# A last product in two column halves: its second pass split into two runs by token halves, and the final scaling of the output spread over GpSimd and ScalarE

## The chip, the cores and the metric

The kernel runs on one core of a Trainium2 chip. The metric is the device time of one execution in microseconds, smaller is better, given as the median of the runs. The change is judged against the kernel before.

## What is computed

One layer of a hybrid encoder for 512 tokens of width 2048: an RMS norm, one wide input projection, a sparse attention branch and a state-space branch, both gated and merged, then the output projection with the residual, and a final RMS norm. The change touches only the last two lines:

```python
def rms_norm(x, g):
    xf = x.astype(jnp.float32)
    y = xf * lax.rsqrt(jnp.mean(xf * xf, axis=-1, keepdims=True) + EPS)
    return (y * g.astype(jnp.float32)).astype(x.dtype)
...
    mixed = gates[:, :, 0] * y_a + gates[:, :, 1] * y_b
    return x + mixed @ w_out        # (512, 2048) @ (2048, 2048)
...
    return rms_norm(x, g_final)
```

## The kernel before, in words

Everything up to `mixed` streams weights through three slots and is the same in both kernels. "The last product" is `mixed @ w_out`. It is computed for one half of the output columns (1024) after the other. In each half the tokens, the inner dimension and the columns are each cut in two, and the 2x2 block product is made with seven block products instead of eight (Winograd's form): sums of blocks of `mixed` (`sums_of`) and sums of blocks of `w_out` (`w_sums` in HBM, made earlier by GpSimd's transfers) are multiplied, and the seven results are combined. A float32 operand is split in a high part (ScalarE copies it, `high_of_quarters`, L1058) and a low part (VectorE subtracts, `low_of_quarters`, L1570), and every block product of 128 rows by 512 columns is three matmuls (`block_product`, L752 to L754).

A block product has eight steps k over the inner dimension. Four pairs of PSUM banks hold the running results, one bank of a pair for each token tile `tb` (0, 1) of a token half: `a_banks` (shown as banks0), `b_banks` (banks2), `c_banks` (banks4), `d_banks` (banks6). Weights come in quarters of 128x512; a ring holds twelve. SyncE issues the load of a quarter when TensorE is done with the one twelve quarters back (`free_at`), ScalarE and VectorE split it, TensorE uses it. SyncE, ScalarE, VectorE and TensorE each run through the steps n in order, and extra work is hung on certain steps of their queues.

Per column half there is a **first pass**, 8 steps with 3 quarters and 18 matmuls each (into a, b, c), and a **second pass**, 8 steps with 4 quarters and 24 matmuls each (d, a, b, c). At the end of the first pass a is saved (`kept1`) and combined with b and c on VectorE (`mix`: u2, u4). The products a, b and c of the second pass wait for these. `add_shared` adds kept1, u2 and u4 to `res`, which holds x (`load_res`, one of eight loads a step from n = 10 on); it is eight additions on VectorE and stands at step 15 and at step 27. After column half 0 `take_first_half` adds the banks to `res` with ten additions at step 17 (L1596); the first matmul into each bank of column half 1 waits for `bank_taken`.

At the end, tiles of 128 tokens are finished in the order `LAST_TOKENS` = 2, 3, 0, 1. Columns 0 to 1023 of each tile are complete long before; they have been squared and multiplied by g_final. The last two steps run in the order b, d, then a, c, so tiles 2 and 3 are complete 24 matmuls before the end and tiles 0 and 1 at the end. For each tile ScalarE makes sum of squares and square root, VectorE the reciprocal (L1666) and the scaled second column half (`finish`, L1668), GpSimd scales the first column half (L497), and SyncE stores the two halves (L447, L449).

## Time and profile before

| what | value |
|---|---|
| median of 3 runs | 1167.07 us (1166.68 to 1168.58) |
| profiled execution, its own time | 1165.59 us |
| its span, first to last instruction | 1163.7 us |
| TensorE matmuls busy | 1129.8 us, 97% of the span |
| VectorE, ScalarE, GpSimd busy | 728.6, 427.9, 47.1 us |
| chain that ended last | TensorE 83%, VectorE 12%, ScalarE 2% |

An engine's share of busy time is an average. Where TensorE is full, other engines' work costs nothing, and only its gaps and the stretch after its last matmul can be shortened. The last product begins at 995.0 us of the span. Times of rows count from the start of the span.

### The profile page before, as it was taken

The page shows a single profiled execution, that of the slowest core. Times are in us where ns is not written, and L with a number is a line of the kernel's source. Part 1 is how long each engine was busy: PE and PEld are TensorE (multiplying, and loading weights), DVE is VectorE, ACT ScalarE, POOL GpSimd, SP SyncE. Part 2 cuts the span into 40 slices and gives each one's busy share as a digit, 9 for nine tenths or more (in the row PEclk, how much of TensorE's full clock was granted, in tenths as well). Part 3 has the DMA queues.
Part 4 walks back from the last instruction along what each step waited for, and adds up shares of the span by engine and source line. Part 5 has one row for each costly group of instructions (what it writes and reads, how often), then busy time and mean ns, then how long its engine had stood idle before and what let it go on. Part 6 is the DMA issues. An engine that isn't in the chain of part 4 may idle for free.

```text
span 1163.7 us, 13431 instructions
## 1 busy us (share of the span) xinstructions
PE 1129.8 (97%) x5381; PEld 934.4 (80%) x5381; DVE 728.6 (63%) x1227; ACT 427.9 (37%) x563; POOL 47.1 (4%) x48
## 2 busy tenths in 40 slices
PE   5999999999999999999999999999999999999995
PEld 4999888888787788888777777888888888787884
DVE  5887558999646556528768886343234344866576
ACT  7423334332255452223222323333412222744363
POOL 4000000000000000000000000000000000000002
PEclk9999999999999999999999999999999999999998
DMA  7344443556633127565445656354576333578654
GB/s 252 102 116 109 142 148 109 138 116 140 150 109 97 50 76 171 143 134 154 130 122 160 144 127 149 115 179 145 113 165 156 78 103 90 182 241 288 216 187 170
DMA packets 188631, 166.35 MB, mean 143 GB/s; under 512 B 12868, under 2 KB 162712, under 8 KB 187928
## 3 DMA queue, kind: packets, MB, share of 16 engines
q1 hardware_dynamic: 167584, 129.97, 38.3%
q0 software_dynamic: 12800, 33.56, 12.7%
q10 hardware_dynamic: 8184, 1.95, 0.8%
q8 instruction: 43, 0.70, 0.2%
q14 instruction: 20, 0.16, 0.0%
HBM read 159.17 MB, written 37.75 MB: 169 GB/s over the span
## 4 chain that ended last, share of the span: by engine, by line
PE 83%; DVE 12%; ACT 2%; issue 1%; DMA 0%; ACTq 0%; POOL 0%; POOLq 0%; DVEq 0%
PE banks L507 21%; PE banks L508 21%; PE banks L509 21%; PE banks L752 4%; PE banks L753 4%; PE banks L754 4%; DVE w_lo L1154 2%; DVE score L1260 2%; DVE small L1259 2%; PE banks L659 2%; PE banks L640 1%; DVE score L1248 1%; DVE res L1596 1%; PE banks L709 1%; PE banks L649 1%
## 5 line engine op out<-in xcount | busy, mean ns | idle before, releaser
L507 PE MATMUL banks<-act_hi,w_hi 128*128 128x512 f32 (+1 forms) x1088 | 421.6, 388 | 2.7 <-DVE w_lo L1154 2.7
L509 PE MATMUL banks<-act_hi,w_lo 128*128 128x512 f32 (+1 forms) x1088 | 416.8, 383 | 0.0
L508 PE MATMUL banks<-act_lo,w_hi 128*128 128x512 f32 (+1 forms) x1088 | 416.7, 383 | 0.0
L1154 DVE TENSOR_TENSOR w_lo<-w_raw,w_hi 128x2048 fp32r<-128x2048 f32 x80 | 183.1, 2289 | 96.0 <-ACT w_hi L818 95.0
L507 PEld LDWEIGHTS banks<-act_hi,w_hi 128*128 128x128 f32 x1088 | 204.4, 188 | 42.9 <-DVE w_lo L1154 4.3
L509 PEld LDWEIGHTS banks<-act_hi,w_lo 128*128 128x128 f32 x1088 | 204.2, 188 | 38.5
L508 PEld LDWEIGHTS banks<-act_lo,w_hi 128*128 128x128 f32 x1088 | 204.5, 188 | 34.4
L818 ACT ACTIVATE w_hi<-w_raw 128x2048 fp32r<-128x2048 f32 (+1 forms) x81 | 154.2, 1903 | 101.5 <-DMA w_raw<-in_w_in 101.2
L1570 DVE TENSOR_TENSOR w_lo<-w_raw,w_hi 128x512 fp32r<-128x512 f32 (+1 forms) x64 | 68.2, 1088 | 43.6 <-ACT w_hi L1058 43.2
L1058 ACT ACTIVATE w_hi<-w_raw 128x512 fp32r<-128x512 f32 (+1 forms) x64 | 60.0, 951 | 72.6 <-DMA w_raw<-w_sums 48.7
L1583 DVE TENSOR_TENSOR gate<-gate,yb 128x512 f32<-128x512 f32 x16 | 11.1, 692 | 83.0 <-ACT gate L824 83.0
L824 ACT ACTIVATE gate<-banks,g_cols 128x512 f32<-128x512 f32 x16 | 11.0, 688 | 127.8 <-PE banks L509 127.8
L890 ACT ACTIVATE relu<-banks 128x256 f32<-128x256 f32 (+2 forms) x48 | 23.6, 492 | 90.8 <-PE banks L608 84.6
L507 PE MATMUL banks<-a_hi,w_hi 128*128 128x512 f32 x128 | 50.1, 391 | 0.0
L509 PE MATMUL banks<-a_hi,w_lo 128*128 128x512 f32 x128 | 49.8, 389 | 0.0
L508 PE MATMUL banks<-a_lo,w_hi 128*128 128x512 f32 x128 | 49.8, 389 | 0.0
L1248 DVE SCALAR_TENSOR_TENSOR score<-relu,w_idx,score 128x256 f32<-128x256 f32 (+2 forms) x45 | 27.8, 618 | 28.9 <-ACT relu L890 27.6
L754 PE MATMUL banks<-w_hi,ya_r 128*128 128x512 f32 x96 | 37.4, 389 | 0.0
L752 PE MATMUL banks<-w_hi,act_hi 128*128 128x512 f32 x96 | 37.3, 389 | 0.0
L753 PE MATMUL banks<-w_lo,act_hi 128*128 128x512 f32 x96 | 37.3, 389 | 0.0
L909 ACT ACTIVATE probs<-probs,small 128x128 f32<-128x128 f32 (+3 forms) x32 | 18.0, 563 | 42.7 <-DVE small L1352 42.7
L824 ACT ACTIVATE ya<-banks 128x512 f32<-128x512 f32 x16 | 9.6, 597 | 62.2 <-PE banks L509 53.3
(290 smaller groups left out, 1438.4 us busy)
## 6 DMA issues: line engine op xcount, KB each, us to landing
w_raw<-in_w_in SPq DMA_DIRECT2D x68, 1024.0 KB, 5.9
w_sums<-in_w_out POOLq DMA_DIRECT2D x24, 1024.0 KB, 8.4
w_raw<-w_sums SPq DMA_DIRECT2D x32, 512.0 KB, 4.2
w_sums<-w_sums POOLq DMA_DIRECT2D x8, 1024.0 KB, 11.2
w_raw<-in_w_att_out SPq DMA_DIRECT2D x8, 1024.0 KB, 5.5
w_raw<-in_w_out SPq DMA_DIRECT2D x16, 512.0 KB, 4.3
xt<-in_x SPq DMA_DIRECT2D x4, 1024.0 KB, 8.2
w_raw<-in_w_ssm_out SPq DMA_DIRECT2D x4, 1024.0 KB, 5.2
```

The lines of the kernel that those rows point to most:

```text
L507: nc.tensor.matmul(out_ap, wh, x_hi[k], start=(j == 0), stop=False)
L508: nc.tensor.matmul(out_ap, wh, x_lo[k], start=False, stop=False)
L509: last = nc.tensor.matmul(out_ap, wl, x_hi[k], start=False, stop=(j == n - 1))
L752: nc.tensor.matmul(bank[:, :], m_hi, hi_ring[:, w], start=(k == 0), stop=False)
L753: nc.tensor.matmul(bank[:, :], m_hi, lo_ring[:, w], start=False, stop=False)
L754: return nc.tensor.matmul(bank[:, :], m_lo, hi_ring[:, w], start=False, stop=(k == HALF_K - 1))
L818: nc.scalar.activation(w_hi[:, u % SLOTS, 0:n_el], w_raw[:, u % SLOTS, 0:n_el], ACT.Copy).then_inc(high_done, 1)
L890: nc.scalar.activation(relu[:, n % 2, 0:(b + 1) * P], pair_bank[n % 2][:, 0:(b + 1) * P], ACT.Relu, scale=IDX_DIM ** -0.5).then_inc(relu_d ...
L1058: nc.scalar.activation(hi_ring[:, part], raw_ring[:, part], ACT.Copy).then_inc(q_high, 1)
L1154: v.tensor_tensor(w_lo[:, u % SLOTS, :], w_raw[:, u % SLOTS, :], w_hi[:, u % SLOTS, :].bitcast(F32), ALU.subtract).then_inc(split_done, 1)
L1248: ins = v.scalar_tensor_tensor(scores[b], r, w, scores[b], ALU.mult, ALU.add)
L1570: v.tensor_tensor(lo_ring[:, part], raw_ring[:, part], hi_ring[:, part].bitcast(F32), ALU.subtract).then_inc(q_split, 1)
```

## The change

Steps are renumbered: each column half now has three **runs** of eight steps, named (half, run, k) here. Run 0 is the first pass as before. Run 1 has 2 quarters a step and makes the products of d and b, which belong to tiles 2 and 3; its steps go in pairs, d of both, then b of both. Run 2 has 2 quarters a step and makes a and c, which belong to tiles 0 and 1; in its last two steps all products of tile 0 come first and then all of tile 1. What hung on steps is hung on new ones: `load_res` on (0,1,4) to (0,2,3), `add_shared` on (0,2,1) and (1,1,3), the additions of d and b (`take_late_tokens`, six) on (half,2,4), those of a and c of column half 0 (`take_early_tokens`, four) on (1,0,1), ScalarE's means and square root table on (1,1,6), the finishing of tiles 2 and 3 on (1,2,5) and (1,2,6). The first step of column half 1 starts with b instead of a. The first column half of the last tile (tile 1) is scaled by ScalarE (`scale_half`), the other three by GpSimd as before. The number of matmuls, of bytes loaded and of bytes stored stays the same.

```diff
+def step_at(n):
+
+    half, run, k = n // (3 * HALF_K), n // HALF_K % 3, n % HALF_K
+    return half, run, k
...
-    return half * 7 * HALF_K + (3 * HALF_K + 4 * k if second else 3 * k)
+    half, run, k = step_at(n)
+    return half * 7 * HALF_K + (3 * k, 3 * HALF_K + 2 * k, 5 * HALF_K + 2 * k)[run]
...
-    return ((0, 2), (2, 4)) if block_at(n)[1] else ((0, 1), (1, 3))
+    return ((0, 2),) if step_at(n)[1] else ((0, 1), (1, 3))
...
+        def first_order(half, k):
+
+            return (1, 0, 2) if (half, k) == (1, 0) else (0, 1, 2)
...
-                if which == 1 - second:
-                    source = w_sums[half, k, :, 2 * second:2 * second + 2, :].rearrange("p i n -> p (i n)")
+                if which or run == 1:
+                    source = w_sums[half, k, :, 2 * run:2 * run + 2, :].rearrange("p i n -> p (i n)")
...
-                if 10 <= n < 18:
-                    if n == 10:
+                if 12 <= n < 20:
+                    if n == 12:
                         sp.wait_ge(m_low, 2 * HALF_K)
-                    load_res((n - 10) // TOK, (n - 10) % TOK)
-                if n == 3 * HALF_K:
-                    sp.wait_ge(q_done, done_at(2 * HALF_K + QUADS - 1, 2, 1))
+                    load_res((n - 12) // TOK, (n - 12) % TOK)
+                if n == 4 * HALF_K:
+                    sp.wait_ge(q_done, done_at(3 * HALF_K + QUADS - 1, 2, 1))
...
-            for i, t in enumerate(LAST_TOKENS):
+            for i, t in enumerate(LAST_TOKENS[:-1]):
                 pool.wait_ge(scale_ready, i + 1)
```
```diff
+            pe.wait_ge(tile_free, TILE0["out"])
+            for half in range(2):
+                n0 = half * 3 * HALF_K
+                for k in range(HALF_K):
+                    if half == 0:
+                        pe.wait_ge(m_low, SPLIT_ORDER.index((0, k)) + 1)
+                    for part in first_order(half, k):
+                        wait_quarter(n0 + k, part)
                         for tb in range(2):
-                            second_pass(n, i, tb).then_inc(q_done, 1)
+                            first_run(n0 + k, part, tb)
+                n0 += HALF_K
+                for k0 in range(0, HALF_K, 2):
+                    for part in range(2):
+                        for k in (k0, k0 + 1):
+                            if half == 0:
+                                pe.wait_ge(m_low, SPLIT_ORDER.index((1, k)) + 1)
+                            wait_quarter(n0 + k, part)
+                            for tb in range(2):
+                                second_run(n0 + k, part, tb)
+                n0 += HALF_K
+                for k in range(HALF_K - 2):
+                    wait_quarter(n0 + k, 0)
+                    for part in range(2):
+                        for tb in range(2):
+                            third_run(n0 + k, part, tb)
+                for tb in range(2):
+                    for k in (HALF_K - 2, HALF_K - 1):
+                        wait_quarter(n0 + k, 0)
+                        for part in range(2):
+                            third_run(n0 + k, part, tb)
```
```diff
             high_of_first(4)
 
+            def scale_half(i):
+                t = LAST_TOKENS[i]
+                act.wait_ge(scale_ready, i + 1)
+                act.wait_ge(first_scaled, 2 * TOK)
+                act.wait_ge(final_done, i)
+                nc.scalar.activation(res[:, t, 0:HALF], res[:, t, 0:HALF], ACT.Copy, scale=small[:, 188 + t:189 + t]
+                                     ).then_inc(final_done, 1)
...
+            def root_of(i):
+                t = LAST_TOKENS[i]
+                act.wait_ge(part_ready, i + 1)
+                link(nc.scalar.activation(square_out[:, 0:2, :].rearrange("p a n -> p (a n)"), res[:, t, HALF:D], ACT.Square,
+                                          accum_out=small[:, 176 + t:177 + t]))
+                nc.scalar.activation(small[:, 184 + t:185 + t], small[:, 176 + t:177 + t], ACT.Sqrt, bias=small[:, 180 + t:181 + t],
+                                     scale=1.0 / D).then_inc(squares_done, 1)
...
+                if half and run == 1 and k == 6:
+                    act.wait_ge(first_squared, 2 * TOK)
+                    for t in range(TOK):
+                        link(mean_of(t))
+                    link(nc.scalar.activation(small[:, 176:177], small[:, 163:164], ACT.Sqrt))
+                if half and run == 2 and k in (5, 6):
+                    root_of(k - 5)
+            for i in (2, 3):
+                root_of(i)
+            scale_half(3)
```
```diff
-            def take_first_half():
-
-                n = 2 * HALF_K - 1
-                dve.wait_ge(shared_added, 8)
+            def finished(half, run, part, tb):
+
+                dve.wait_ge(q_done, done_at(3 * HALF_K * half + HALF_K * run + HALF_K - 1, part, tb))
+
+            def take_late_tokens(half):
+
+                dve.wait_ge(shared_added, 8 * half + 8)
+                col = half * HALF
                 for tb in range(2):
-                    dve.wait_ge(q_done, done_at(n, 1, tb))
-                    add_part(tb, 0, a_banks[tb]).then_inc(bank_taken, 1)
+                    finished(half, 1, 0, tb)
+                    part = add_part(2 + tb, col, d_banks[tb])
+                    if half == 0:
+                        part.then_inc(bank_taken, 1)
+                    else:
+                        link(part)
                 for tb in range(2):
-                    dve.wait_ge(q_done, done_at(n, 2, tb))
-                    add_part(2 + tb, 512, b_banks[tb])
-                    add_part(2 + tb, 0, b_banks[tb], ALU.subtract).then_inc(bank_taken, 1)
-                for tb in range(2):
-                    dve.wait_ge(q_done, done_at(n, 3, tb))
-                    add_part(tb, 512, c_banks[tb]).then_inc(bank_taken, 1)
-                for tb in range(2):
-                    dve.wait_ge(bank_taken, 3 + tb)
-                    add_part(2 + tb, 0, d_banks[tb]).then_inc(bank_taken, 1)
```
```diff
+                    finished(half, 1, 1, tb)
+                    add_part(2 + tb, col + 512, b_banks[tb])
+                    if half == 0:
+                        dve.wait_ge(bank_taken, tb + 1)
+                    add_part(2 + tb, col, b_banks[tb], ALU.subtract).then_inc(part_ready if half else bank_taken, 1)
+
+            def take_early_tokens(half, tb):
+
+                finished(half, 2, 0, tb)
+                part = add_part(tb, half * HALF, a_banks[tb])
+                if half == 0:
+                    part.then_inc(bank_taken, 1)
+                finished(half, 2, 1, tb)
+                add_part(tb, half * HALF + 512, c_banks[tb]).then_inc(part_ready if half else bank_taken, 1)
+
+            def inverse_root(i):
+
+                t = LAST_TOKENS[i]
+                dve.wait_ge(squares_done, i + 1)
+                v.reciprocal(small[:, 188 + t:189 + t], small[:, 184 + t:185 + t]).then_inc(scale_ready, 1)
+
+            def finish(i):
+
+                t = LAST_TOKENS[i]
+                dve.wait_ge(scale_ready, i + 1)
+                v.scalar_tensor_tensor(res[:, t, HALF:D], res[:, t, HALF:D], small[:, 188 + t:189 + t], g_last[:, HALF:D], ALU.mult, ALU.mult
+                                       ).then_inc(final_rest_done, 1)
...
+                if run == 2 and k == 4:
+                    take_late_tokens(half)
+                if (half, run, k) == (1, 0, 1):
+                    for tb in range(2):
+                        take_early_tokens(0, tb)
+                if half and run == 1 and k >= HALF_K - 2:
...
-            for tb in range(2):
-                add_part(2 + tb, HALF, last_bank(tb, 0)).then_inc(part_ready, 1)
-            finish(0)
-            for tb in range(2):
-                add_part(tb, HALF, last_bank(tb, 1)).then_inc(part_ready, 1)
-            for tb in range(2):
-                add_part(tb, HALF + 512, last_bank(tb, 3)).then_inc(part_ready, 1)
-            for i in range(1, TOK):
-                finish(i)
+                if half and run == 2 and k in (5, 6):
+                    inverse_root(k - 5)
+                    finish(k - 5)
+            take_early_tokens(1, 0)
+            inverse_root(2)
+            take_early_tokens(1, 1)
+            finish(2)
+            inverse_root(3)
+            finish(3)
```

How the order of instructions changes, at three places. TensorE, the first matmul into each bank of column half 1 (two more of the same bank follow each):

```order
L752 MATMUL banks0<-w_hi_53,ya_r_102 128x512 [waits bank_taken,q_split]
...
L752 MATMUL banks0<-w_hi_53,ya_r_102 128x512 [waits bank_taken]
...
L752 MATMUL banks2<-w_hi_53,s_hi_111 128x512 [waits bank_taken,q_split]
...
L752 MATMUL banks2<-w_hi_53,s_hi_111 128x512 [waits bank_taken]
...
L752 MATMUL banks4<-w_hi_53,s_hi_111 128x512 [waits bank_taken,q_split]
...
L752 MATMUL banks4<-w_hi_53,s_hi_111 128x512 [waits bank_taken]
```

and in the changed kernel:

```order
L768 MATMUL banks2<-w_hi_53,s_hi_111 128x512 [waits bank_taken,q_split]
...
L768 MATMUL banks2<-w_hi_53,s_hi_111 128x512 [waits bank_taken]
...
L768 MATMUL banks0<-w_hi_53,ya_r_102 128x512 [waits bank_taken,q_split]
...
L768 MATMUL banks0<-w_hi_53,ya_r_102 128x512 [waits bank_taken]
...
L768 MATMUL banks4<-w_hi_53,s_hi_111 128x512 [waits bank_taken,q_split]
...
L768 MATMUL banks4<-w_hi_53,s_hi_111 128x512 [waits bank_taken]
```

b's banks come first and a's second. SyncE's queue, around the first loads of res (w_raw is the ring of weights), before:

```order
L428 DMA w_raw_51<-w_sums 128x1024 [waits q_done]
L428 DMA w_raw_51<-in_w_out 128x1024 [waits q_done]
L431 DMA res_100<-in_x 128x1024 [waits m_low]
L428 DMA w_raw_51<-w_sums 128x1024 [waits q_done]
L428 DMA w_raw_51<-in_w_out 128x1024 [waits q_done]
L431 DMA res_100<-in_x 128x1024
```

and changed:

```order
L444 DMA w_raw_51<-w_sums 128x1024 [waits q_done] x6
L447 DMA res_100<-in_x 128x1024 [waits m_low]
L444 DMA w_raw_51<-w_sums 128x1024 [waits q_done]
L447 DMA res_100<-in_x 128x1024
L444 DMA w_raw_51<-w_sums 128x1024 [waits q_done]
L447 DMA res_100<-in_x 128x1024
```

A load of res now follows each load of two quarters, where it followed each second one. VectorE's last instructions (banks0, 2, 4, 6 are a, b, c, d; squares_done is a wait on ScalarE), before:

```order
L1596 TENSOR_TENSOR res_100<-res_100,banks6 128x512 [waits q_done]
L1666 RECIPROCAL small_58<-small_58 128x1 [waits squares_done]
L1668 SCALAR_TENSOR_TENSOR res_100<-res_100,small_58,g_last_113 128x1024 [waits scale_ready]
L1596 TENSOR_TENSOR res_100<-res_100,banks0 128x512 [waits q_done] x2
L1596 TENSOR_TENSOR res_100<-res_100,banks4 128x512 [waits q_done] x2
L1666 RECIPROCAL small_58<-small_58 128x1 [waits squares_done]
L1668 SCALAR_TENSOR_TENSOR res_100<-res_100,small_58,g_last_113 128x1024 [waits scale_ready]
```

and changed:

```order
L1619 TENSOR_TENSOR w_lo_52<-w_raw_51,w_hi_53 128x1024 [waits q_high]
L1705 RECIPROCAL small_58<-small_58 128x1 [waits squares_done]
L1711 SCALAR_TENSOR_TENSOR res_100<-res_100,small_58,g_last_113 128x1024 [waits scale_ready]
...
L1645 TENSOR_TENSOR res_100<-res_100,banks0 128x512 [waits q_done]
L1645 TENSOR_TENSOR res_100<-res_100,banks4 128x512 [waits q_done]
L1705 RECIPROCAL small_58<-small_58 128x1 [waits squares_done]
L1645 TENSOR_TENSOR res_100<-res_100,banks0 128x512 [waits q_done]
L1645 TENSOR_TENSOR res_100<-res_100,banks4 128x512 [waits q_done]
L1711 SCALAR_TENSOR_TENSOR res_100<-res_100,small_58,g_last_113 128x1024 [waits scale_ready]
L1705 RECIPROCAL small_58<-small_58 128x1 [waits squares_done]
L1711 SCALAR_TENSOR_TENSOR res_100<-res_100,small_58,g_last_113 128x1024 [waits scale_ready]
```

The finishing of tiles 2 and 3 stands between the splits of weights, that of tile 0 between the additions of tile 1.

## Rows read from the trace of the kernel before

**Rows 1.** Page: busy us, share of span, instructions of each engine.

```profile
PE 1129.8 (97%) x5381; PEld 934.4 (80%) x5381; DVE 728.6 (63%) x1227; ACT 427.9 (37%) x563; POOL 47.1 (4%) x48
```

**Rows 2.** Timeline (start us, us, what, [idle before]): TensorE, the last matmuls.

```profile
1145.05 0.39 PE L752 MATMUL banks<-w_hi,act_hi 128*128 128x512 f32 x1
...
1149.58 0.39 PE L754 MATMUL banks<-w_hi,act_lo 128*128 128x512 f32 x1
```

**Rows 3.** Timeline: TensorE where column half 0 ends and half 1 begins.

```profile
1071.13 0.39 PE L754 MATMUL banks<-w_hi,act_lo 128*128 128x512 f32 x1
1072.66 0.47 PE L752 MATMUL banks<-w_hi,ya_r 128*128 128x512 f32 x1 [1.15 <-DVE res L1596]
...
1076.37 0.39 PE L752 MATMUL banks<-w_hi,s_hi 128*128 128x512 f32 x1
```

**Rows 4.** Timeline: VectorE before and at that turn.

```profile
1063.33 1.29 DVE L1619 TENSOR_TENSOR res<-res,kept 128x512 f32<-128x512 f32 x2
1064.53 3.69 DVE L1619 TENSOR_TENSOR res<-res,u 128x512 f32<-128x512 f32 x6
...
1071.83 6.06 DVE L1596 TENSOR_TENSOR res<-res,banks 128x512 f32<-128x512 f32 x10
```

**Rows 5.** Timeline: GpSimd in the tail.

```profile
1151.37 6.32 POOL L497 TENSOR_SCALAR res<-res,small 128x1024 f32<-128x1024 f32 x3 [1.56 <-DVE small L1666]
```

**Rows 6.** Timeline: SyncE queue, the last output transfer issued.

```profile
1158.11 1.00 SPq L449 DMA_DIRECT2D out_dram<-res  x1
```

**Rows 7.** Timeline: SyncE queue, three issues of weights.

```profile
1033.47 0.45 SPq L428 DMA_DIRECT2D w_raw<-in_w_out  x1
...
1049.79 0.33 SPq L428 DMA_DIRECT2D w_raw<-in_w_out  x1
...
1121.44 0.33 SPq L428 DMA_DIRECT2D w_raw<-w_sums  x1
```

**Rows 8.** Timeline: ScalarE, the copies that wait for these weights.

```profile
1038.40 1.06 ACT L1058 ACTIVATE w_hi<-w_raw 128x1024 fp32r<-128x1024 f32 x1 [0.89 <-DMA w_raw<-in_w_out]
...
1056.49 1.06 ACT L1058 ACTIVATE w_hi<-w_raw 128x1024 fp32r<-128x1024 f32 x1 [1.66 <-DMA w_raw<-in_w_out]
...
1125.28 1.06 ACT L1058 ACTIVATE w_hi<-w_raw 128x1024 fp32r<-128x1024 f32 x1 [0.94 <-DMA w_raw<-w_sums]
```

**Rows 9.** Timeline: VectorE, one split and two multiplications by g_last.

```profile
1115.53 1.22 DVE L1570 TENSOR_TENSOR w_lo<-w_raw,w_hi 128x1024 fp32r<-128x1024 f32 x1 [2.48 <-ACT w_hi L1058]
...
1129.24 2.35 DVE L1654 TENSOR_TENSOR res<-res,g_last 128x1024 f32<-128x1024 f32 x2
```

**Rows 10.** Timeline: VectorE in the tail.

```profile
1147.33 0.16 DVE L1666 RECIPROCAL small<-small 128x1 f32<-128x1 f32 x1 [1.00 <-ACT small L1109]
1147.53 1.28 DVE L1668 SCALAR_TENSOR_TENSOR res<-res,small,g_last 128x1024 f32<-128x1024 f32 x1
1148.73 2.47 DVE L1596 TENSOR_TENSOR res<-res,banks 128x512 f32<-128x512 f32 x4
...
1152.84 1.82 DVE L1668 SCALAR_TENSOR_TENSOR res<-res,small,g_last 128x1024 f32<-128x1024 f32 x1
...
1154.76 1.95 DVE L1668 SCALAR_TENSOR_TENSOR res<-res,small,g_last 128x1024 f32<-128x1024 f32 x1
```

**Rows 11.** Timeline: ScalarE, table load and the tail.

```profile
1139.75 1.28 ACT L1122 ACT_TABLE_LOAD   x1
...
1145.82 1.06 ACT L1114 ACTIVATE square_out<-res 128x1024 f32<-128x1024 f32 x1 [4.58 <-DVE res L1596]
...
1147.01 0.29 ACT L1109 ACTIVATE small<-small 128x1 f32<-128x1 f32 x1
```

**Rows 12.** Windows: stretch, length, busy by engine, PEclk, DMA share, GB/s.

```profile
1049.90:1052.60 2.70, 2.70 (x14) 2.23 (x13) 1.54 (x2) 1.06 (x1) 0.00 (x0) 1.00 0.92 231
...
1058.10:1060.80 2.70, 2.70 (x14) 2.23 (x13) 1.42 (x2) 1.06 (x1) 0.00 (x0) 1.00 0.94 358
...
1033.60:1069.00 35.40, 35.40 (x158) 29.33 (x157) 18.45 (x21) 12.94 (x13) 0.00 (x0) 1.00 0.86 290
```

## What the change will do to the time

> **What bounds the kernel now.** The first view to read is the page's line of busy times: TensorE is busy for 97% of the span [rows 1]. The last product cannot shrink, since the change leaves its 672 matmuls as they are; only places where TensorE stands still, and what follows its last matmul, can give time back. So the second view is TensorE's timeline. In the last product the matmuls start at an even pace: from 1145.05 to 1149.58 us lie 20 starts, 0.2265 us each [rows 2]. One place breaks it. Where the first column half ends and the second begins, the last old matmul starts at 1071.13 and the first matmul of c_banks at 1076.37 us [rows 3]. Between them lie 12 matmuls (six for a_banks, six for b_banks; the trace lacks a record of some), so 13 steps or 2.94 us at the pace, and 5.24 us have passed: 2.3 us are lost. The row of 1072.66 names VectorE at L1596, which empties the banks. VectorE's own row says why: ten additions in one piece, begun only at 1071.83 [rows 4].
>
> The third view is the end. The last matmul starts at 1149.58 and lasts 0.39, so it ends at E = 1149.97 us. The span ends at 1163.7, 13.7 us later. In that tail GpSimd's three scalings stand in a row from 1151.37 to 1157.69, 2.1 us each, and the last two output transfers are issued behind them, the very last at 1158.11 [rows 5, 6]. From the start of the last issue to the end of the span it is 5.6 us. The tail before is thus 8.14 us of computing and issuing, and 5.6 us of transfer.
>
> **The turn between the halves.** The change lets b_banks be finished and emptied in the run before (d and b are complete 21.7 us earlier), and only a and c are left for the turn. VectorE must do four additions at the turn instead of ten (10 x 0.61 = 6.06 us, so 0.61 each [rows 4]), and TensorE first works six matmuls (1.36 us) into b_banks, which are long free. The product for a_banks[0] is finished 15 matmuls (3.4 us) before the turn, for c_banks[0] 2.7 us, since tile 0 goes first in the last two steps. The four additions wait in VectorE's order only behind the split of step (1,0,1), whose quarters come free two and a half steps before the turn; their transfer, copy and subtraction end about 1.5 us before the turn, by 3.8 us of landing, 1.06 and 1.23 [rows 7 to 9]. Additions from -1.5 on leave a_banks[0] free at about -0.9 and a_banks[1] at about +0.6, both before they are wanted at +1.4 and +2.0; c_banks[1], its product done at 0, is free at 1.2 and wanted at 3.4. Gain: 2.3 us, all of it on the path; bounds 0 (VectorE comes late, below) and 2.3.
>
> **The end.** Tile 1 is the last 12 matmuls, so tile 0 is complete at E - 2.72. From there, with durations of [rows 10, 11]: addition 0.69, to E - 2.03; on ScalarE square, read of the sum and root, from 1145.82 to 1147.30, 1.48, and 0.06 to get there, to E - 0.49; reciprocal with its gaps 0.19, to E - 0.30. VectorE then adds the two banks of tile 1, 0.62 each (2.47 for four), to E + 0.94; ScalarE's square and root take 1.54, to E + 2.48. Meanwhile VectorE finishes tile 0, which takes 1.28, or 1.82 to 1.95 where GpSimd was already running: the two long rows are those that begin inside GpSimd's stretch from 1151.37 on [rows 5, 10]. In the new order GpSimd starts on tile 0 at about E - 0.2 and is busy until E + 2, so I take 1.95, to E + 2.9. Reciprocal to E + 3.1, last multiplication 1.28 (GpSimd is idle by then) to E + 4.4. The last tile's first half is on ScalarE beside it: the trace has no such scaling, its nearest row is the 128x1024 copy of 1.06 us [rows 8], the upper bound GpSimd's 2.1 us; with 1.06 it is ready at E + 4.2, issued, and the other half is issued at E + 4.6. Then 5.6 us: E + 10.2 instead of E + 13.7, **3.5 us** saved. Had the multiplication of tile 0 taken 1.28, it would be 3.9; with a scaling of 2.1 us the issue waits to E + 5.6 and 2.5 are left.
>
> The Trainium skill ("SBUF — State Buffer", section on the two separate sides) says of the two long rows that a VectorE instruction with two SBUF inputs and a GpSimd instruction take the port pair as an exclusive lock, and the later one waits to the end of the other. The trace agrees here: 1.82 ends 1.18 us after GpSimd's second scaling begins at about 1153.5. The rule speaks against the change at another place, which is the rival on GpSimd below.
>
> **What gets tighter in between.** The second pass of 4 quarters a step becomes two runs of 2 quarters, 12 matmuls or 2.72 us a step. Three things that were hung on steps now come twice as densely.
>
> The eight loads of res, one per step, lay 5.44 us apart beside 1 MB of weights, and now lie 2.72 us apart beside 0.52 MB: 1.05 MB in 2.72 us is 386 GB/s wanted for 21.8 us, where it was 289. The queue gave 290 GB/s at a share of 0.86 over that stage, which is 337 at full share, and 358 in its best window [rows 12]. The 8.39 MB take 23.4 to 24.9 us, so they fall behind by 1.7 to 3.1 us. What absorbs it: the step most at risk is (0,2,2), because VectorE runs the eight additions of add_shared(0) ahead of its split. The load of (0,2,1) is issued some 15.9 us before TensorE wants (0,2,2). Behind its landing come ScalarE's copy 1.06, the split 1.23, the eight additions 4.89 (1063.33 to 1068.22), the next split 1.23 and hand-overs, 8.6 us [rows 4, 8, 9]. So landing, from issue to ScalarE's start, may take 7.3 us. Before it took 3.8 us undisturbed (1121.44 to 1125.28) and up to 6.7 beside res (1049.79 to 1056.49); 4.9 near the start of that stage (1033.47 to 1038.40) [rows 7, 8]. Adding the lag to 4.9 gives 6.6 to 8.0: a stall of 0 to 0.9 us. Adding it to 6.7 gives up to 2.8. I take **0.5 us**, near the first, since 6.7 already holds part of the queueing, and keep 0 and 2.8.
>
> VectorE's work in run 1 of the second half is 8 splits, mix (4 additions, 2.5), add_shared (4.9) and four multiplications by g_last (2.35 for two [rows 9]): about 22 us in 21.8. It starts some 5 us ahead and ends about 3 ahead, as the late additions come in run 2. ScalarE has there a copy (1.06) and two squares a step (one of double width took 1.06, with read-outs to add), about 2.4 of 2.72 us, and then the square root's table load, 1.28 us [rows 11]. Both hold; price 0. The finishing of tiles 2 and 3 (6 additions, 2 multiplications, 2 output transfers) moves under matmuls: price 0 as long as the split of step (1,2,7) comes in time.
>
> **Sum.** -2.3 (turn) - 3.5 (end) + 0.5 (new stall) = -5.3 us. The profiled execution goes from 1165.59 (span 1163.7) to about 1160.3 (span 1158.4). It lies 1.5 us under the median of 1167.07, which I move by the same amount: **1161.8 us**.
>
> **The rivals.** *The loads fall further behind.* If landing takes 8.5 to 10 us beside res, TensorE stops for 1.2 to 2.8 us around (0,2,0) to (0,2,2): 1167.07 - 5.8 + 2.3 = 1163.6. For it: 6.7 us of landing at a lower demand. Against: windows of 358 GB/s. *GpSimd in the stream.* Two scalings now run at about E - 11 and E - 8, and VectorE's splits of (1,2,6) and (1,2,7) may each wait 0.9 us for their end, as the long rows did. Without it the split of (1,2,7) is ready about 2 us before it is wanted, with it about 0.2 us; a little lateness elsewhere makes it a stall of up to 1 us: 1162.4. The sentence of the skill above gives this result too. *The turn does not open.* VectorE reaches the four additions only after the turn, because late loads or add_shared hold its queue; the 2.3 us stay: 1164.1. *Slower.* In one window the queue moved 231 GB/s at a share of 0.92 [rows 12], 251 at full share. If mixing x, weights and sums at this density runs the whole stage so, 8.39 MB take 33.4 us, 11.6 more than the matmuls; less the 2.4 us of room (7.3 - 4.9), TensorE stops for 9.2 us, and the result is 1167.07 - 5.8 + 9.2 = 1170.5. It decides from a lag of 10.5 us on, which is a rate under 260 GB/s held for the whole stage.
>
> **How the numbers follow.** Forecast 0.50; loads further behind 0.26; GpSimd in the stream 0.12; turn not opened 0.08; slower 0.04. A measurement of this kernel tells about 0.2%, 2.3 us, from no change, so faster means under 1164.7. All of the forecast and of GpSimd's case lie there, nearly all of the first rival and half of the third: 0.88 faster, 0.08 the same, 0.04 slower. The range is 1159.5 to 1164.4. Its low end is no stall, 3.9 at the end, and 0.7 of a last transfer that meets less traffic, with the spread of the runs. Its high end takes in the first rival.
>
> **What would show it.** Right: no gap of TensorE at the turn; a last output issue 4.6 us after the last matmul; the two finishing steps of tiles 2 and 3 under matmuls. Wrong: a wait of TensorE for VectorE's split in steps (0,2,0) to (0,2,2), with landings over 7.3 us; splits of about 2 us beside GpSimd; four additions begun after the turn.

## The result, and the profile after

| what | before | after |
|---|---|---|
| median of 6 runs each | 1167.01 us (1166.26 to 1168.58) | 1159.09 us (1158.32 to 1159.86) |
| ratio, 95% interval | | 0.9931 [0.9918, 0.9944] |
| profiled execution, its own time | 1165.59 us | 1158.73 us |
| its span | 1163.7 us | 1156.8 us |

The kernel is 7.9 us faster. The prediction had 1161.8 us and a range from 1159.5; the time is 0.4 us under it. The mechanisms it named are there, and one term of the sum was too large: the 5.6 us from the last output issue to the end of the span, kept as before. It measures 4.26.

**The page of after.** TensorE's busy time hardly moves against [rows 1], the span is shorter:

```profile
PE 1129.0 (98%) x5381; PEld 934.6 (81%) x5381; DVE 728.1 (63%) x1227; ACT 428.2 (37%) x562; POOL 46.1 (4%) x47
```

**The turn.** The timeline of TensorE after, where [rows 3] had the stall. The last old matmul starts at 1071.79, the first of b_banks (operand s_hi) 0.23 later, and at 1073.38 a_banks follows at the same pace. No row carries an idle time:

```profile
1071.79 0.39 PE L770 MATMUL banks<-w_hi,act_lo 128*128 128x512 f32 x1
1072.02 0.39 PE L768 MATMUL banks<-w_hi,s_hi 128*128 128x512 f32 x1
...
1073.38 0.39 PE L768 MATMUL banks<-w_hi,ya_r 128*128 128x512 f32 x1
```

VectorE after, against [rows 4]: two of the four additions are done before the turn, two end at 1072.9.

```profile
1069.87 1.28 DVE L1645 TENSOR_TENSOR res<-res,banks 128x512 f32<-128x512 f32 x2
1071.54 1.37 DVE L1645 TENSOR_TENSOR res<-res,banks 128x512 f32<-128x512 f32 x2 [0.39 <-PE banks L770]
```

**Where the stall was feared.** The load of step (0,2,1), its copy on ScalarE, then VectorE with add_shared and the split of (0,2,2); below them windows of that stage (columns as in [rows 12]). Landing, from issue to ScalarE's start, took 6.8 us (1039.57 to 1046.36), against 7.3 allowed. The queue moved 350 GB/s over 21.4 us and 398 in its best window, and TensorE was busy for all 21.40 us.

```profile
1039.57 0.33 SPq L444 DMA_DIRECT2D w_raw<-in_w_out  x1
```
```profile
1046.36 1.06 ACT L1110 ACTIVATE w_hi<-w_raw 128x1024 fp32r<-128x1024 f32 x1 [1.76 <-DMA w_raw<-in_w_out]
```
```profile
1049.79 3.69 DVE L1668 TENSOR_TENSOR res<-res,u 128x512 f32<-128x512 f32 x6
1053.40 3.52 DVE L1619 TENSOR_TENSOR w_lo<-w_raw,w_hi 128x1024 fp32r<-128x1024 f32 x3
```
```profile
1033.60:1055.00 21.40, 21.40 (x96) 17.72 (x95) 12.46 (x15) 7.68 (x8) 0.00 (x0) 1.00 0.97 350
1038.30:1041.00 2.70, 2.70 (x14) 2.23 (x13) 1.19 (x1) 0.66 (x1) 0.00 (x0) 1.00 1.05 398
```

**The tail.** VectorE after, against [rows 10]: the multiplication of tile 0 takes 1.28, not 1.95. GpSimd after, against [rows 5]: two scalings lie in the stream, one in the tail. Then the output transfers issued by SyncE; four of the eight now leave under matmuls.

```profile
1147.97 1.26 DVE L1645 TENSOR_TENSOR res<-res,banks 128x512 f32<-128x512 f32 x2
1149.15 1.28 DVE L1711 SCALAR_TENSOR_TENSOR res<-res,small,g_last 128x1024 f32<-128x1024 f32 x1
...
1150.97 1.28 DVE L1711 SCALAR_TENSOR_TENSOR res<-res,small,g_last 128x1024 f32<-128x1024 f32 x1
```
```profile
1136.48 6.30 POOL L513 TENSOR_SCALAR res<-res,small 128x1024 f32<-128x1024 f32 x2 [248.69 <-DVE small L1705]
1148.15 1.12 POOL L513 TENSOR_SCALAR res<-res,small 128x1024 f32<-128x1024 f32 x1 [5.37 <-DVE small L1705]
```
```profile
1143.18 0.43 SPq L465 DMA_DIRECT2D out_dram<-res  x1
1149.29 0.33 SPq L463 DMA_DIRECT2D out_dram<-res  x1
1150.46 0.33 SPq L465 DMA_DIRECT2D out_dram<-res  x1
1152.15 0.33 SPq L463 DMA_DIRECT2D out_dram<-res  x1
1152.54 0.42 SPq L465 DMA_DIRECT2D out_dram<-res  x1
```

Set piece by piece, profile against profile (E is the end of the last matmul, 1149.97 and 1148.34):

| piece | before | after | difference | forecast |
|---|---|---|---|---|
| first matmul of the last product | 995.02 | 995.70 | +0.68 | 0 |
| from it to the last matmul's start | 154.56 | 152.25 | -2.31 | -2.3, +0.5 |
| E to the last output issue | 8.14 | 4.20 | -3.94 | -3.5 |
| last output issue to the end | 5.59 | 4.26 | -1.33 | 0 |
| sum | | | -6.90 | -5.3 |

The first line is no effect of the change: in the nine kernels below that don't touch that start it lies between 995.07 and 996.53. The last 1.0 us between -6.9 and the medians' -7.9 is the luck of the two profiled executions: before, it lies 1.4 us under the median of six, after 0.4 under.

### The profile page after: what moved, and what is told of

It reads as the page before. It is cut to its first block, busy times and chain, and to the rows that moved or that the text cites. A ratio compares the mean times of both kernels' runs of the same rounds, so it can differ in the third digit from the quotient of the medians.

```text
span 1156.8 us, 13435 instructions
## 1 busy us (share of the span) xinstructions
PE 1129.0 (98%) x5381; PEld 934.6 (81%) x5381; DVE 728.1 (63%) x1227; ACT 428.2 (37%) x562; POOL 46.1 (4%) x47
## 3 DMA queue, kind: packets, MB, share of 16 engines
q10 hardware_dynamic: 8184, 1.95, 0.8%
## 4 chain that ended last, share of the span: by engine, by line
PE 84%; DVE 12%; ACT 1%; DMA 1%; issue 1%; SPq 0%; DVEq 0%; ACTq 0%
PE banks L523 21%; PE banks L524 21%; PE banks L525 21%; PE banks L768 4%; PE banks L769 4%; PE banks L770 4%; DVE w_lo L1203 2%; DVE score L1309 2%; DVE small L1308 2%; PE banks L675 2%; PE banks L656 1%; DVE score L1297 1%; DMA xt<-in_x 1%; PE banks L725 1%; PE banks L665 1%
```

## The experiments

Each is after or before with one edit. "Before", run again beside them, had medians of 1166.34 to 1167.18 us, so a median is good to some 0.8 us, and each ratio is to the "before" run beside it. Therefore the pieces of the table above are read too, which scatter less: three kernels with the same end have tails (E to the end of the span) of 8.44 to 8.49 us. "The stream" is the second line of the table, from the first matmul of the last product to the start of its last one.

### The turn: the six additions put back

```diff
-                if run == 2 and k == 4:
+                if half and run == 2 and k == 4:
...
                 if (half, run, k) == (1, 0, 1):
+                    take_late_tokens(0)
```

> The changed kernel, with the six additions of d and b of column half 0 put back to the turn, ahead of those of a and c. Theory (the 2.3 us of the turn were ten additions in one piece on VectorE): VectorE comes to them about 2.2 us before the turn and needs 0.61 us each; b_banks[1] is free 0.5 us late, a_banks[1] and c_banks[1] once more, in all a stall of TensorE of 1 to 1.5 us, so 1160.1 to 1160.6 us. Rival (the stall came from late weights of the second pass): no wait of TensorE for VectorE at the turn, 1159.1.

Measured 1160.68 us, ratio to before 0.9947 [0.9932, 0.9962]; the stream takes 154.00 us, 1.75 more than after, where 1 to 1.5 were expected. TensorE's timeline has the stall back, in three parts, and names VectorE's additions:

```profile
1071.57 0.39 PE L770 MATMUL banks<-w_hi,act_lo 128*128 128x512 f32 x1
1072.51 0.47 PE L768 MATMUL banks<-w_hi,s_hi 128*128 128x512 f32 x1 [0.55 <-DVE res L1645]
...
1073.61 0.50 PE L768 MATMUL banks<-w_hi,s_hi 128*128 128x512 f32 x1 [0.18 <-DVE res L1645]
...
1075.40 0.50 PE L768 MATMUL banks<-w_hi,ya_r 128*128 128x512 f32 x1 [0.15 <-DVE res L1645]
```

So splitting the additions carries 1.75 of the 2.31 us. The other 0.56 doesn't come back with them: here VectorE begins its ten additions at 1069.89, ahead of the turn, and in the kernel before it began them at 1071.83, behind it [rows 4]. That is due to the rest of the change, and no run takes it apart.

### The turn: order a, b, c as before

```diff
-            return (1, 0, 2) if (half, k) == (1, 0) else (0, 1, 2)
+            return (0, 1, 2)
```

> The changed kernel, with the first step of column half 1 in the old order a, b, c. Theory (four additions are few enough): a_banks[0] is free 1.6 us before the turn, a_banks[1] about 0.1 us after it and wanted 0.7 us after it, so no wait: 1159.1, 0 to +0.3. Rival (the order b first carries the gain of the turn): TensorE waits for a, +0.7 to +1.4 us.

Measured 1158.63 us, 0.9931 [0.9916, 0.9946], stream 152.26 us, no gap. The order is worth nothing once only four additions stand at the turn: a_banks are empty in time without it. The prediction counted six matmuls of room that were not needed. No run has the order b first beside ten additions.

### The end: last two steps in plain order

```diff
-                for k in range(HALF_K - 2):
+                for k in range(HALF_K):
...
-                for tb in range(2):
-                    for k in (HALF_K - 2, HALF_K - 1):
-                        wait_quarter(n0 + k, 0)
-                        for part in range(2):
-                            third_run(n0 + k, part, tb)
```

> The changed kernel, with the last two steps of each run 2 in plain order (a for both tiles, then c for both), so that tile 0 is complete 0.7 us before the end instead of 2.7. Theory: ScalarE's square and root of tile 0 (1.5 us) then lie after the last matmul and VectorE's queue holds the additions of tile 1 behind them: the last output issue goes from 4.2 to about 6.1 us after the last matmul, +1.9 us, 1161.0; the turn stays without a stall. Rival (the tail was shortened by tiles 2 and 3 alone): within 0.4 us of the changed kernel.

`done_at`, which counts TensorE's finished products, is changed to match. Measured 1160.98 us, 0.995 [0.9935, 0.9965]. The last issue comes at E + 6.24, the end 4.25 later; the tail is 2.0 us longer than after. Tile 0 before tile 1 is worth its 2 us.

### The end: the fourth scaling on GpSimd

```diff
-            for i, t in enumerate(LAST_TOKENS[:-1]):
+            for i, t in enumerate(LAST_TOKENS):
...
-            scale_half(3)
```

> The changed kernel, with the first half of the last tile scaled on GpSimd again. Theory (a GpSimd instruction and a VectorE instruction with two SBUF inputs exclude each other): GpSimd waits for the multiplication of 1.28 us and then works 1.1 us, so its row is about 2.4 us long, the last output issue is 5.4 us after the last matmul instead of 4.2: +1.2 us, 1160.3. Rival (GpSimd works beside VectorE, 1.12 us as in the one undisturbed row): 0 to +0.2 us.

Measured 1159.91 us, 0.9943 [0.9927, 0.996]. GpSimd's row for the last tile, against 1.12 us for tile 0:

```profile
1150.36 1.28 DVE L1710 SCALAR_TENSOR_TENSOR res<-res,small,g_last 128x1024 f32<-128x1024 f32 x1
1150.42 2.21 POOL L513 TENSOR_SCALAR res<-res,small 128x1024 f32<-128x1024 f32 x1 [1.77 <-DVE small L1704]
```

It begins 0.06 us after VectorE's multiplication and ends 1.0 us after it. The last issue goes to E + 5.32, the end 3.95 later: the tail is 0.8 us longer than after. ScalarE's scaling is worth that much, since GpSimd would have to stand behind VectorE.

### The scaling on ScalarE alone, in the kernel before

```diff
-            for i, t in enumerate(LAST_TOKENS):
+            for i, t in enumerate(LAST_TOKENS[:-1]):
...
+            act.wait_ge(scale_ready, TOK)
+            act.wait_ge(final_done, TOK - 1)
+            nc.scalar.activation(res[:, t_last, 0:HALF], res[:, t_last, 0:HALF], ACT.Copy, scale=small[:, 188 + t_last:189 + t_last]
+                                 ).then_inc(final_done, 1)
```

> The kernel before, with only the first half of the last tile scaled on ScalarE. Theory: ScalarE is ready 1.15 us after the last reciprocal (1154.75), the last multiplication on VectorE still ends at about 1156.7, since it waits for GpSimd's second scaling, and the last issue comes at about 1156.9 instead of 1158.1: -1.2 us, 1165.8. Rival (nothing is won as GpSimd's third scaling ends as late as before the fourth did): 0 to -0.3 us.

Measured 1166.39 us beside 1166.66 for before, 0.9998 [0.9988, 1.0008]: nothing. ScalarE has its row late, since final_done made it wait for GpSimd's third scaling. But its result was ready at 1158.0, which is E + 6.9, 0.8 us sooner after the last matmul than GpSimd's fourth in before (E + 7.7). The two last issues came with 0.86 and 1.16 us each, where most take 0.33 to 0.43, and the end 5.76 us after the last. The tail is 13.6 us against 13.7. So the rival's figure came true (0 to -0.3), though work had been taken out:

```profile
1156.85 1.15 ACT L1137 ACTIVATE res<-res,small 128x1024 f32<-128x1024 f32 x1 [2.19 <-POOL res L497]
...
1158.03 0.86 SPq L447 DMA_DIRECT2D out_dram<-res  x1
1158.94 1.16 SPq L449 DMA_DIRECT2D out_dram<-res  x1
```

### GpSimd almost without work, in the kernel before

GpSimd scales 8 of 1024 columns of each tile; the others of the first half stay unscaled.

```diff
-                pool.tensor_scalar(res[:, t, 0:HALF], res[:, t, 0:HALF], small[:, 188 + t:189 + t], 1.0, ALU.mult, ALU.mult).then_inc(final_done, 1)
+                pool.tensor_scalar(res[:, t, 0:8], res[:, t, 0:8], small[:, 188 + t:189 + t], 1.0, ALU.mult, ALU.mult).then_inc(final_done, 1)
```

> The kernel before, with GpSimd scaling only 8 of the 1024 columns of each first half (the rest of these columns is left unscaled). Theory (exclusion): all four multiplications of VectorE take 1.28 us, none 1.82 or 1.95, and the last issue comes at about 1155.7, 5.7 us after the last matmul instead of 8.1: -2.4 us, 1164.6. Rival (the long rows come from the output transfers that read SBUF at that time): the third and fourth multiplication stay at 1.8 to 1.95 us, and 1.1 us less is won.

Measured 1165.79 us, 0.9997 [0.9987, 1.0006]. VectorE's multiplications all take 1.28 to 1.29, so the 1.82 and 1.95 of [rows 10] were GpSimd's doing. GpSimd's rows of 8 columns take 1.28 to 1.38 each:

```profile
1153.02 1.28 DVE L1668 SCALAR_TENSOR_TENSOR res<-res,small,g_last 128x1024 f32<-128x1024 f32 x1
1153.08 1.36 POOL L497 TENSOR_SCALAR res<-res,small 128x8 f32<-128x8 f32 x1 [2.42 <-DVE small L1666]
...
1157.75 0.89 SPq L447 DMA_DIRECT2D out_dram<-res  x1
1158.69 1.17 SPq L449 DMA_DIRECT2D out_dram<-res  x1
```

Each ends some 0.15 us behind VectorE's row, which it would by waiting for it. All is computed at 1157.2, E + 5.5, but the issues stretch again, to E + 7.01, and the end is 5.91 behind: the last issue was expected at E + 5.7, and the tail is only 0.8 us shorter than before, of 2.2 us by which the computing ends sooner. Two kernels now had work taken out of the tail and kept 0.1 of 0.8 and 0.8 of 2.2 us, and in both the queue's share was 1.01 to 1.03 from 1156 to 1162.

### Tile 0's output transfers left out, in the kernel before

The two transfers of tile 0 are not made, so its rows of the output are missing.

```diff
             for i, t in enumerate(LAST_TOKENS):
+                if i == 2:
+                    continue
...
```

> The kernel before, without the two output transfers of the third tile (its rows are not written). Theory (the last transfer is slow because up to 2 MB are written in 2.4 us): from the start of the last issue to the end of the span 4.3 us instead of 5.6, -1.3 us, 1165.7. Rival (a fixed cost of the last transfer and its wait): 5.4 to 5.6 us, no change.

Measured 1165.64 us, 0.9991 [0.9981, 1.0]: at the edge of the noise, so the pieces are read. With 1 MB less ahead of it the last transfer takes 4.59 us from issue to end, not 5.59; 4.3 was expected, and 5.4 to 5.6 by the rival. The last issue comes at E + 8.13, as in before, so the tail is 1.0 us shorter. At 400 GB/s the 1 MB would be 2.6 us: only 1.0 of it lay on the path, and 4.59 us remain although the queue's share was only 0.43 from 1158 to 1160.

### The stores of tiles 2 and 3 held to the end, in the kernel after

```diff
+            sp.wait_ge(squares_done, 3)
             for i, t in enumerate(LAST_TOKENS):
                 sp.wait_ge(final_done, i + 1)
```

> The changed kernel, with the four output transfers of tiles 2 and 3 held back until the root of tile 0 is made, about 0.45 us before the last matmul ends; all else is left. Theory (the last transfer takes as long as the stores in flight ahead of it need): all eight stores, 4.19 MB, then leave in the tail. In both kernels' traces the queue moves some 400 GB/s when it is full, from about 1.6 us after the first issue: 10.5 us of transfer, so the span ends some 12 to 13 us after the last matmul, with the last issue unchanged at 4.2 us: 8 to 9 us from issue to end in place of 4.26, and a median some 4 us above the changed kernel's 1159.1, near 1163. Rival (the last transfer has a duration of its own, and 5.6 against 4.3 is scatter): issue to end stays 4.3 to 5.6 and the median within 1.3 us of 1159.1.

Measured 1162.75 us, 0.9963 [0.995, 0.9977]; the tail is 12.15 us, 3.7 more than after, though all rows of VectorE, ScalarE and GpSimd in it take and stand as after. The queue's windows and the last issues:

```profile
1149.00:1151.00 2.00, 0.00 (x0) 0.00 (x0) 1.84 (x3) 1.29 (x3) 0.68 (x1) 1.00 0.95 381
1151.00:1153.00 2.00, 0.00 (x0) 0.00 (x0) 1.45 (x2) 1.31 (x2) 0.00 (x0) 0.54 1.02 403
...
1157.00:1159.00 2.00, 0.00 (x0) 0.00 (x0) 0.00 (x0) 0.00 (x0) 0.00 (x0) 0.50 1.04 418
1159.00:1160.90 1.90, 0.00 (x0) 0.00 (x0) 0.00 (x0) 0.00 (x0) 0.00 (x0) 0.50 0.26 101
```
```profile
1153.76 1.18 SPq L464 DMA_DIRECT2D out_dram<-res  x1
1154.98 1.37 SPq L466 DMA_DIRECT2D out_dram<-res  x1
```

Eight stores, 4.19 MB, leave at 381 to 418 GB/s without a pause, and the end comes 1.9 us behind the last full window. One detail was expected otherwise: the delay is split between slower issues (last at E + 6.23, expected 4.2) and the rest (5.92, expected 8 to 9). The sum, 12.15, is within the 12 to 13 expected. The rival, a duration of its own with scatter, had 4.3 to 5.6 and a median within 1.3 us of after: both are missed, so it can't account for the difference. A part that doesn't depend on the backlog is left, though. The bytes that the windows show between the last issue and the end separate the two:

| kernel | last issue to end, us | MB moved in it | us at 400 GB/s | rest, us |
|---|---|---|---|---|
| before | 5.59 | 1.65 | 4.1 | 1.5 |
| before, GpSimd almost without work | 5.91 | 1.78 | 4.5 | 1.4 |
| before, tile 0's transfers left out | 4.59 | 1.06 | 2.6 | 2.0 |
| after | 4.26 | 1.12 | 2.8 | 1.5 |
| after, fourth scaling on GpSimd | 3.95 | 1.05 | 2.6 | 1.3 |
| after, stores held | 5.92 | 1.83 | 4.6 | 1.3 |

The last two transfers alone are 1.05 MB. Before and after differ by 0.54 MB of earlier stores, 1.3 us at 400 GB/s, which is the whole 1.33. The rest of 2.0 in the third line is not explained.

With this the windows of **before** read differently than I read them:

```profile
1154.00:1156.00 2.00, 0.00 (x0) 0.00 (x0) 1.97 (x3) 0.00 (x0) 2.00 (x2) 0.50 0.79 320
1156.00:1158.00 2.00, 0.00 (x0) 0.00 (x0) 0.71 (x1) 0.00 (x0) 1.69 (x1) 0.50 1.02 408
1158.00:1160.00 2.00, 0.00 (x0) 0.00 (x0) 0.00 (x0) 0.00 (x0) 0.00 (x0) 0.50 1.02 397
1160.00:1162.00 2.00, 0.00 (x0) 0.00 (x0) 0.00 (x0) 0.00 (x0) 0.00 (x0) 0.50 1.02 408
1162.00:1163.70 1.70, 0.00 (x0) 0.00 (x0) 0.00 (x0) 0.00 (x0) 0.00 (x0) 0.50 0.14 53
```

The queue is full from 1156 to 1162, and the last issue at 1158.11 takes 1.00 us [rows 6]. From 1156 on the store queue sets the end, and GpSimd's pace lies at most 1.0 us behind it, since that is all that leaving out 1 MB gained. The tail after is full only for a while: 370 GB/s from 1151.0 to 1154.5.

### Twice the traffic beside res, in the kernel after

Eight additional transfers of 0.5 MB from HBM to HBM, each behind a load of res.

```diff
                     load_res((n - 12) // TOK, (n - 12) % TOK)
+                    sp.dma_start(scratch[n - 12], x_v[(n - 12) % TOK][:, (n - 12) // TOK * HALF:((n - 12) // TOK + 1) * HALF]).then_inc(extra_done, 16)
...
```

> The changed kernel, with each of the eight loads of res followed by a copy of the same 0.5 MB from HBM to HBM, which nobody uses. Theory (the queue can give about 365 GB/s there and the changed kernel wants 386 for 21.8 us, just bearable): 12.6 MB need 34.5 us, the lag of 12.7 us exceeds the room by 7 to 10 us, and TensorE waits for VectorE's splits in runs 1 and 2 of column half 0: 1166 to 1169. Rival (the queue has much more to give than its windows showed): a stall below 3 us.

Measured 1167.56 us, 1.0007 [0.9998, 1.0016]; the stream takes 161.64 us, 9.4 more than after. TensorE waits for splits at the places named, first here:

```profile
1053.30 0.39 PE L774 MATMUL banks<-w_hi,act_lo 128*128 128x512 f32 x1
1056.01 0.62 PE L772 MATMUL banks<-w_hi,act_hi 128*128 128x512 f32 x1 [2.32 <-DVE w_lo L1623]
1056.43 0.63 PE L773 MATMUL banks<-w_lo,act_hi 128*128 128x512 f32 x1
...
1059.76 0.39 PE L772 MATMUL banks<-w_hi,act_lo 128*128 128x512 f32 x1
```

The same stretch in which after moved 350 GB/s shows the queue at its limit here:

```profile
1033.60:1055.00 21.40, 20.09 (x89) 16.10 (x87) 5.26 (x6) 5.30 (x5) 0.00 (x0) 1.00 1.01 385
```

The rival of lagging loads is thus a real mechanism, and the changed kernel stands below the point from which it bites. How far below, one run with doubled traffic does not say.

### A further step: the first product on free banks, and a finer last tile

After, TensorE still idles at the start of the last product, until ScalarE has copied the last gate tile out of PSUM banks that of the new product only a_banks take over (0.84 us, the one wait it has left there):

```profile
994.48 0.39 PE L525 MATMUL banks<-act_hi,w_lo 128*128 128x512 f32 x1
995.70 0.50 PE L768 MATMUL banks<-w_hi,ya_r 128*128 128x512 f32 x1 [0.84 <-ACT gate L876]
```

```diff
-            return (1, 0, 2) if (half, k) == (1, 0) else (0, 1, 2)
+            return (1, 0, 2) if k == 0 else (0, 1, 2)
...
-            pe.wait_ge(tile_free, TILE0["out"])
...
                         wait_quarter(n0 + k, part)
+                        if n0 + k + part == 0:
+                            pe.wait_ge(tile_free, TILE0["out"])
```

> The changed kernel, with the order b, a, c also at the first step of column half 0, and TensorE's wait for the last gate copy moved from ahead of the first product to ahead of the first one for a_banks. The trace of the changed kernel shows 1.22 us between the last matmul before and the first of the last product, 0.84 of them waiting for the gate copy of ScalarE; the pace is 0.23. If only the shared banks hold TensorE there, the gap goes to 0.23 and the median falls by 1.0 us. Rival: the operand sums of the first step are then late, the gap moves behind the first six matmuls, and the median stays within 0.3 us.

Measured 1158.19 us, 0.9924 [0.9911, 0.9937]. The gap is gone (0.23 us from the last old matmul to the first of b_banks):

```profile
995.33 0.39 PE L525 MATMUL banks<-act_hi,w_lo 128*128 128x512 f32 x1
995.56 0.39 PE L768 MATMUL banks<-w_hi,s_hi 128*128 128x512 f32 x1
```

By the trace that is 1.0 us; the ratios, 0.9924 against 0.9931, say 0.8 but their intervals overlap. Its median is the lowest of the kernels here.

The second kernel adds this to it (SyncE stores each of the two pieces when it is done, and ScalarE's queue stores the last tile's first half):

```diff
-            finish(3)
+            t = LAST_TOKENS[3]
+            dve.wait_ge(scale_ready, 4)
+            for j in range(2):
+                c = HALF + 512 * j
+                v.scalar_tensor_tensor(res[:, t, c:c + 512], res[:, t, c:c + 512], small[:, 188 + t:189 + t], g_last[:, c:c + 512],
+                                       ALU.mult, ALU.mult).then_inc(final_rest_done, 1)
...
```

> e10 with a finer end: the last tile's scaling on VectorE in two pieces of 512 columns, each stored when done, and its first column half stored from ScalarE's own queue. By the chain of computing alone the last issue comes 0.2 to 0.4 us earlier relative to the last matmul and carries half the bytes: 0.3 to 0.6 us less than e10. By the theory of stores in flight (the queue is full at 400 GB/s from 1151.0 to 1153 in the changed kernel's trace, and 2.1 MB leave in its tail whatever the order), less comes out: 0 to 0.3 us.

Measured 1158.29 us, 0.9927 [0.9914, 0.994]: the same as e10. The tail is 8.51 us against 8.46, though the work is handed over in finer pieces. The chain of computing alone had promised 0.3 to 0.6, the theory of stores in flight 0 to 0.3. It fits the second better, without proving it for this case alone.

## Why the prediction was right and wrong, step by step

- **The turn, -2.3: right, to 0.01 us.** The stream is 2.31 shorter, and with the additions put back 1.75 return. Of the reasons given, the four additions carry these 1.75; the order b, a, c carries nothing beside them; 0.56 is left to the rest of the change.
- **New stall, +0.5 (0 to 2.8): too high, it was 0.** The mechanism was reckoned well: landing was 6.8, within the 6.6 to 8.0 worked out and under the 7.3 allowed, and the 350 GB/s of the stage lie within the 337 to 358 taken. The choice in the range was too high. At 350 GB/s the lag is 2.2 us and landing 7.1, so no stall; and the top ends were added up too high, 8.0 less 7.3 is 0.7 and not 0.9, 9.8 less 7.3 is 2.5 and not 2.8. The windows of before were also no measure of the capacity, since the queue was not asked for more there: it reached 398 in one window after, and 385 over the whole stretch with doubled traffic.
- **Computing in the tail, -3.5: a little small, -3.94.** What was off is the multiplication of tile 0, taken at 1.95 for GpSimd beside it. GpSimd started at 1148.15, while VectorE was adding out of PSUM, and was done 1.12 us later, before it mattered: the row is 1.28. It is then off the path: the last reciprocal waits 0.35 us for ScalarE's root of tile 1. My own alternative for that case was 3.9. GpSimd's 2.1 us a tile before were about half waiting: in after and in the run with the fourth scaling on GpSimd its row is 1.12 where VectorE's rows beside it read a PSUM bank, and 2.21 where it begins behind a multiplication of 1.28.
- **Transfer after the last issue, 5.6 kept: the term that was mis-sized, it is 4.26.** This is the step that failed: I took the 5.6 us as a fixed price behind the last issue, whatever was in the queue. Only some 4.3 of them are that. The rest was 0.6 MB of earlier stores still in a full queue, which had 4.19 MB to move from E on; the change puts 2.1 MB of these under matmuls and leaves 0.07 MB of earlier stores at the last issue. I had allowed 0.7 us for it at the low end of the range and called it traffic; it was 1.33. Leaving out 1 MB before takes 1.0 us off (4.59), and the stores held to the end bring it back (5.92).
- **GpSimd in the stream (rival): the mechanism exists, the price is 0.** Its two scalings took 6.30 us together, and one multiplication of VectorE was stretched to 1.87. The splits behind took 1.21 to 1.22, and TensorE never waited. Mostly it was GpSimd that stood back:

```profile
1136.33 1.28 DVE L1711 SCALAR_TENSOR_TENSOR res<-res,small,g_last 128x1024 f32<-128x1024 f32 x1
1137.53 1.22 DVE L1619 TENSOR_TENSOR w_lo<-w_raw,w_hi 128x1024 fp32r<-128x1024 f32 x1
...
1138.86 1.87 DVE L1711 SCALAR_TENSOR_TENSOR res<-res,small,g_last 128x1024 f32<-128x1024 f32 x1
1140.66 1.21 DVE L1619 TENSOR_TENSOR w_lo<-w_raw,w_hi 128x1024 fp32r<-128x1024 f32 x1
```

- **Loads further behind, and slower (rivals): not here.** Doubled traffic produces the stalls, 9.4 us in all; the rate that the slower case needed, under 260 GB/s over the stage, was not near (350).
- **The step to the median.** I moved the median by the same amount as the profile and said that the profiled run of before lies 1.5 us under it. The one after lies only 0.4 under. This adds 1.0 us to what the pieces give, and no view of one execution could have shown it. It is luck, and so is the 0.7 us by which the last product begins later: the start of before, 995.02, is the earliest of all eleven kernels with this start. The three pieces that the change touches make -7.6 us, or 1159.5, which is the low end of the range; the last 0.4 us below it are the two pieces of luck together.

The sum of misses against the forecast: stall -0.5, computing -0.4, transfer -1.3, start of the stage +0.7, profiled run against median -1.1: -2.6, and 1161.8 - 2.6 is the 1159.1 measured (0.1 is rounding).

## What to carry to other kernels

When the end of a kernel stores much, look at the queue's windows before counting the chain of computing: if the share stays at 1.0 up to the last microseconds, faster arithmetic is largely given back in the queue, as in two of the runs here, and having fewer bytes left at the last issue brings the end nearer. Not byte for byte: the chain of computing may follow close behind, as when 1 MB less gained 1.0 us and not 2.6. Spreading work that empties shared buffers so that only what depends on the last product stands at a turn carried at least three quarters of the stall here (1.75 of 2.31 us), and the order of use added nothing to that once the buffers were free in time. Take an engine's cost from a row that stood alone, and a queue's capacity from a stretch in which it was full.

## What the runs showed of the hardware

- A GpSimd row contains its wait for VectorE. The same scaling of 128x1024 shows 1.12, 2.1, 2.21 and 3.15 us (6.30 for two), and one of 128x8 shows 1.28 to 1.38, each as VectorE's multiplications around it allow. The Trainium skill ("SBUF — State Buffer", section on the two separate sides) has the exclusive lock, and that whichever starts second waits; the rows agree. Here that was mostly GpSimd: VectorE's rows grew by 0.5 to 0.7 us, GpSimd's by 1 to 2.
- An issue on SyncE takes 0.33 to 0.43 us in most rows, but 0.79 to 1.37 in the tail of the run with the stores held, where the share is 0.95 to 1.04. A long issue is a hint of a backlog that can be read without any window, no more: among the loads of after, at a share of 0.97, one takes 0.88 and the others that have a row of their own 0.32 to 0.43.
- The queue moved 397 to 418 GB/s at a share of 1.01 to 1.04 with stores, and 398 with mixed loads. The Trainium skill ("Perfetto Trace Analysis", section Roofline) says that a core may pull more than its share of 358 GB/s when it is the only active one of its pair, up to a ceiling near 435 set by its 16 DMA engines; these windows agree. By that sentence the 386 GB/s wanted are within reach, and the stall of +0.5 would have been estimated at 0.
- TensorE's matmuls came 0.43 us apart after the 2.3 us stall in the run with doubled traffic, in place of 0.23, until 1059.4. The granted clock of that stretch, 0.53 in the window below, is nearly all at the lower of its two levels (1.2 GHz). It had been fully busy up to 1053.3 and idle for 2.3 us before that, so the stall cost about 1.7 us (nine steps take 3.75 us, from 1056.01 to 1059.76, where the pace gives 2.04) more than its own length. At the turn of the kernel before, where TensorE was idle for 1.15 us [rows 3], the granted clock was 1.00 from 1070 to 1080, so no part of its 2.3 us is a lower clock.

```profile
1056.00:1059.50 3.50, 3.49 (x9) 2.71 (x10) 3.50 (x7) 1.06 (x1) 0.00 (x0) 0.53 0.92 269
```
